# Third layer of a hybrid transformer on one core: attention heads issued in pairs, and negated scores in all layers

## What is computed

```python
def _masked_softmax(s, mask):
    s = jnp.where(mask, s.astype(jnp.float32), NEG_INF)
    m = jnp.max(s, axis=-1, keepdims=True)
    e = jnp.where(mask, jnp.exp(s - m), 0.0)
    return e / jnp.maximum(jnp.sum(e, axis=-1, keepdims=True), 1e-30)

def second_block(x, ...):
    ...
        h = _rms_norm(x, g_pre_mix[l]) * (1.0 + sc_m) + sh_m
        y = _hybrid_mixer(h, cos, sin, w_in[l], ...)
        x = x + ga_m * _rms_norm(y, g_post_mix[l])
        h = _rms_norm(x, g_pre_ffn[l]) * (1.0 + sc_f) + sh_f
        x = x + ga_f * _rms_norm(_swiglu(h, w_gate_up[l], w_down[l]), g_post_ffn[l])
```

## Time and profile before

| | us |
|---|---|
| median of 3 runs | 1135.73 |
| lowest, highest | 1133.7, 1137.04 |
| the profiled execution, its span | 1136.34, 1134.5 |

### The profile page before, as it was taken

The page is one execution under the profiler, slowest core; times in us unless marked ns, Lnnn a source line. Parts: engine busy times, 40 slices in busy tenths (PEclk is TensorE's granted clock), DMA queues, the critical chain, the costliest instruction groups (busy, mean ns, idle before and its releaser), DMA issues.

```text
span 1134.5 us, 16103 instructions
## 1 busy us (share of the span) xinstructions
PE 1039.9 (92%) x6560; PEld 926.6 (82%) x6560; DVE 684.4 (60%) x1268; ACT 446.4 (39%) x699; POOL 48.0 (4%) x70
## 2 busy tenths in 40 slices
PE   6999869999999899977999999889989859999997
PEld 5877659999988888756999988688766649999986
DVE  3656565777755755456777774756754555555543
ACT  4445323333333355423433333354444354333332
POOL 5100010000000200001000000100000000000000
PEclk9998998999999999898999999989987988999999
DMA  8733028998854553205999864454320025666551
GB/s 269 231 132 111 1 75 260 276 271 246 282 188 125 174 185 120 67 22 167 276 278 261 268 234 165 136 179 149 112 75 1 1 75 149 186 185 186 186 185 38
DMA packets 191706, 185.09 MB, mean 163 GB/s; under 512 B 7130, under 2 KB 161013, under 8 KB 191632
## 3 DMA queue, kind: packets, MB, share of 16 engines
q1 hardware_dynamic: 188576, 175.85, 50.4%
q0 software_dynamic: 2768, 7.87, 2.4%
q10 hardware_dynamic: 288, 0.33, 0.1%
HBM read 182.97 MB, written 1.06 MB: 162 GB/s over the span
## 4 chain that ended last, share of the span: by engine, by line
PE 79%; DVE 12%; ACT 5%; issue 2%; POOL 1%; DMA 1%; SPq 0%; DVEq 0%; POOLq 0%; ACTq 0%
PE ps L979 14%; PE ps L1020 11%; PE ps L1021 11%; PE ps L1022 11%; PE ps L1337 5%; PE ps L957 4%; PE ps L958 4%; PE ps L959 4%; PE ps L1064 3%; DVE wl L1694 3%; PE ps L1074 2%; ACT wh L1455 1%; DVE probs L1907 1%; DMA raw<-in_w_in 1%; ACT probs L1479 1%
## 5 line engine op out<-in xcount | busy, mean ns | idle before, releaser
L1694 DVE TENSOR_TENSOR wl<-raw,wh 128x2048 fp32r<-128x2048 f32 (+5 forms) x147 | 319.6, 2177 | 212.9 <-ACT wh L1455 212.7
L1455 ACT ACTIVATE wh<-raw 128x2048 fp32r<-128x2048 f32 (+5 forms) x147 | 268.1, 1824 | 438.1 <-PE ps L1022 247.6
L1020 PE MATMUL ps<-xh,wh 128*128 128x256 f32 x1056 | 303.1, 287 | 3.3 <-DVE xl L1712 2.0
L1021 PE MATMUL ps<-xl,wh 128*128 128x256 f32 x1056 | 302.0, 286 | 0.0
L1022 PE MATMUL ps<-xh,wl 128*128 128x256 f32 x1056 | 301.8, 286 | 0.0
L1020 PEld LDWEIGHTS ps<-xh,wh 128*128 128x128 f32 x1056 | 206.1, 195 | 4.4 <-issue 4.4
L1021 PEld LDWEIGHTS ps<-xl,wh 128*128 128x128 f32 x1056 | 206.1, 195 | 0.0
L1022 PEld LDWEIGHTS ps<-xh,wl 128*128 128x128 f32 x1056 | 206.0, 195 | 0.0
L957 PE MATMUL ps<-wh,xh 128*128 128x384 f32 (+5 forms) x284 | 106.2, 374 | 12.8 <-DVE wl L1694 7.1
L959 PE MATMUL ps<-wh,xl 128*128 128x384 f32 (+5 forms) x284 | 100.0, 352 | 0.0
L958 PE MATMUL ps<-wl,xh 128*128 128x384 f32 (+5 forms) x284 | 100.0, 352 | 0.0
(11 more groups left out here) (260 smaller groups left out, 1219.5 us busy)
## 6 DMA issues: line engine op xcount, KB each, us to landing
raw<-in_w_down SPq DMA_DIRECT2D x33, 1024.0 KB, 5.0
adaw<-in_w_ada SPq DMA_DIRECT2D x24, 1024.0 KB, 7.1
raw<-in_w_gate SPq DMA_DIRECT2D x44, 512.0 KB, 4.2
raw<-in_w_up SPq DMA_DIRECT2D x44, 512.0 KB, 5.5
raw<-in_w_gate_up SPq DMA_DIRECT2D x44, 512.0 KB, 5.1
raw<-in_w_in SPq DMA_DIRECT2D x12, 768.0 KB, 4.6
raw<-in_w_in SPq DMA_DIRECT2D x8, 1024.0 KB, 5.2
raw<-in_w_o SPq DMA_DIRECT2D x8, 1024.0 KB, 4.9
```

Source lines behind the costliest of these rows:

```text
L1020: mm(o, a[:, v, k, :], xh[:, k, :], start=k == 0, stop=False)
L1021: mm(o, a[:, v, k, :], xl[:, k, :], start=False, stop=False)
L1455: me.go(activation(wh[:, m % NW, 0:n], raw[:, ITEM[item] % NRAW, 0:n], ACT.Copy), wh_ready)
L1694: me.go(V.tensor_tensor(wl[:, m % NW, 0:n], raw[:, ITEM[item] % NRAW, 0:n], wh[:, m % NW, 0:n].bitcast(F32), ALU.subtract), wl_ready)
```

## The change

Third layer: jobs of the first two groups alternate between the two key heads (0, 4, 1, 5, 2, 6, 3, 7), so that two neighbouring jobs read partitions 0 to 63 and 64 to 127. A stage "S2" makes the scores of two jobs, the first row block of both and then the second of both, in banks 4 and 0. The transposes of odd jobs go to bank 2 (jobs below 8) or 1. `pair(p)` adds S2 of pair p, V of the two jobs of pair p-2, whatever stands between, and T of pair p-1. Block 5 is cut into 16 pieces "wq" of three products, spread among the first pairs. The latent group's results go to banks 6 and 7, the output product to banks 2, 3, 0, 1; the window result is now added last. The latent queries' turns go to banks 1 and 0. In all layers `masked` scales by the negative, takes the running minimum and does no negation; `exponents` uses a scale of -1.

```diff
-        for h in range(8):
+        for h in (0, 4, 1, 5, 2, 6, 3, 7):
...
-OBANK = {0: {0: 6, 1: 2, 2: 6}, 1: {0: 6, 1: 2, 2: 6}, 2: {0: 6, 1: 2, 2: 2, 3: 6}}
+OBANK = {0: {0: 6, 1: 2, 2: 6}, 1: {0: 6, 1: 2, 2: 6}, 2: {0: 6, 1: 2, 2: 6, 3: 6}}
...
-YBANK = {0: (0, 1, 2, 3), 1: (0, 1, 2, 3), 2: (0, 1, 6, 7)}
+YBANK = {0: (0, 1, 2, 3), 1: (0, 1, 2, 3), 2: (2, 3, 0, 1)}
...
-    def job(s, jobs=24):
-        add(*((n, k) for n, k in (("T", s - 2), ("V", s - 3), ("S", s)) if 0 <= k < jobs))
+    def fifth(a, b):
+        add(*(("wq", n // 8, n // 4 % 2, n % 4) for n in range(a, b)))
+
+    def pair(p, between=(), jobs=24):
+        if 2 * p < jobs:
+            add(("S2", 2 * p))
+        add(*(("V", k) for k in (2 * p - 4, 2 * p - 3) if k >= 0))
+        add(*between)
+        add(*(("T", k) for k in (2 * p - 2, 2 * p - 1) if 0 <= k < jobs))
...
+    fifth(0, 4)
     add(("wl", "win", 4, 1), ("nT", 0), ("nT", 1), ("top", 1))
...
+    fifth(4, 6)
+    pair(0)
+    fifth(6, 8)
+    add(("wh", "win", 5, 0), ("top", 2))
+    pair(1, [("wq", 1, 0, 0)])
+    fifth(9, 10)
     add(("wl", "win", 5, 0))
...
+    pair(2, [("wq", 1, 0, 2), ("wq", 1, 0, 3)])
+    add(("top", 3))
+    pair(3, [("wq", 1, 1, 0), ("wq", 1, 1, 1)])
+    add(("top", 4))
+    pair(4, [("wq", 1, 1, 2), ("wq", 1, 1, 3)])
+    add(("wh", "win", 5, 1), ("latent_query_rope",), ("cmpS",))
+    pair(5)
+    add(("cmpT",), ("wl", "win", 5, 1), ("out", 0, 0), ("out", 0, 1), ("top", 5))
+    pair(6, [("nT", 2), ("nT", 3)])
+    add(("top", 6), ("top", 7))
+    pair(7, [("cmpV",)])
+    add(("top", 8))
+    pair(8)
+    add(("out", 3, 0), ("out", 3, 1), ("out", 3, 2), ("out", 3, 3))
+    pair(9)
+    add(("out", 1, 0), ("out", 1, 1), ("out", 1, 2), ("out", 1, 3))
+    pair(10)
+    pair(11, [("ht", 0, 0), ("ht", 0, 1)])
+    pair(12, [("wo", 0, 0), ("wo", 1, 0)])
+    pair(13, [("wo", 2, 0), ("wo", 3, 0)])
...
-                put(("nT", a[0]), a[0] - 2, "act")
+                put(("nT", a[0]), 3 - a[0], "act")
...
+            elif stage == "S2":
+                put(("s", L, a[0]), 4, "dve")
+                put(("s", L, a[0] + 1), 0, "dve")
...
-                put(("pt", L, a[0]), 5, turns(L, a[0]))
+                other = L == 2 and a[0] % 2
+                put(("pt", L, a[0]), (2 if a[0] < 8 else 1) if other else 5, turns(L, a[0]))
...
+            def two_scores(k):
+
+                j = JOBS[2][k]
...
+                banks = [claim(("s", 2, k)), claim(("s", 2, k + 1))]
+                for t in range(TT):
+                    for n in range(2):
+                        ins = score(JOBS[2][k + n], banks[n], t)
+                        if t:
+                            fill(ins, ("s", 2, k + n))
...
-                wide = P if not j.last and (j.col + 2) * HD <= 512 else HD
+                wide = P if (j.col + 2) * HD <= 512 and not j.last and (j.kind not in ("slc", "win") or j.col != 3) else HD
...
-                    ins = activation(probs[:, k % 4, a:e], probs[:, k % 4, a:e], ACT.Exp, bias=nmx[:, k % 4, t:t + 1],
+                    ins = activation(probs[:, k % 4, a:e], probs[:, k % 4, a:e], ACT.Exp, bias=mn[:, k % 4, t:t + 1], scale=-1.0,
...
-                    me.go(V.tensor_tensor_reduce(out=probs[:, k % 4, a:e], in0=ps[:, U.bank[key], a:e], in1=mask_of(j, t), scale=j.scale,
-                                                 scalar=-3.4e38, op0=ALU.add, op1=ALU.max, accum_out=mx[:, k % 4, t:t + 1]))
-                me.settle()
-                me.empty(V.tensor_scalar(nmx[:, k % 4, :], mx[:, k % 4, :], -1.0, None, ALU.mult), key)
+                    ins = V.tensor_tensor_reduce(out=probs[:, k % 4, a:e], in0=ps[:, U.bank[key], a:e], in1=mask_of(j, t), scale=-j.scale,
+                                                       scalar=3.4e38, op0=ALU.add, op1=ALU.min, accum_out=mn[:, k % 4, t:t + 1])
+                    if t:
+                        me.empty(ins, key)
+                    else:
+                        me.go(ins)
```

More of the change, by code:

```diff
@@ L941, in first_part, with fifth_part @@
                     mm(o, xh[:, k, 0:P], b[:, k, :], start=False, stop=False)
+            def fifth_part(h, t, k):
+                n = win_width(2, 5)
+                a, b = (w[:, 0:4 * n].rearrange("p (k n) -> p k n", k=4) for w in parts(("win", 2, 5, h)))
+                if h == k == 0:
+                    claim(("win", 2, 5, t))
+                o = ps[:, U.bank["win", 2, 5, t], 0:n]
+                xs = slice(t * P, (t + 1) * P)
+                mm(o, xh[:, 4 * h + k, xs], a[:, k, :], start=h == k == 0, stop=False)
+                mm(o, xh[:, 4 * h + k, xs], b[:, k, :], start=False, stop=False)
+                ins = mm(o, xl[:, 4 * h + k, xs], a[:, k, :], start=False, stop=h == 1 and k == 3)
+                if k == 3:
+                    if h == 1:
+                        fill(ins, ("win", 2, 5, t))
+                    elif t == 1:
+                        leave(ins, ("win", 2, 5, h))
             def win_part(L, i, h, t):
@@ L1046, in scores @@
                 b = claim(("s", L, k))
-                if L == 2 and j.col == 0:
-                    for key in {"slc": (("nT", 0), ("nT", 1), ("nT", 4)), "win": (), "dsa": (("nT", 2), ("nT", 3), ("nT", 7), ("nT", 8))}[j.kind]:
-                        wait_done(pe, key)
-                if k == 0 and L < 2:
+                if k == 0:
                     wait_done(pe, ("ab", L, 0))
@@ L1545, in mixer @@
                 for stage, *a in ORDER[L]:
-                    if stage == "win" and a[1:] == [1, 0]:
+                    if stage == "wq" and a == [1, 0, 3]:
+                        key = ("win", 2, 5, 0)
+                        copy(*win_views(2, 5, 0, win_width(2, 5), U.bank[key]), key)
+                    elif stage == "S2":
+                        exponents(L, a[0])
+                        exponents(L, a[0] + 1)
+                    elif stage == "win" and a[1:] == [1, 0]:
                         key = ("win", L, a[0], 0)
@@ L2178, in mixer @@
                 for stage, *a in ORDER[L]:
-                    if stage == "win" and a[1:] == [1, 1]:
+                    if stage == "wq" and a == [1, 1, 3]:
+                        key = ("win", 2, 5, 1)
+                        copy(*win_views(2, 5, 1, win_width(2, 5), U.bank[key]), key)
+                    elif stage == "S2":
+                        masked(L, a[0])
+                        masked(L, a[0] + 1)
+                    elif stage == "win" and a[1:] == [1, 1]:
                         key = ("win", L, a[0], 1)
```

67 lines of the change are left out of this document (19 added, 48 removed).

## The result

| | before | after |
|---|---|---|
| median of 4 runs, us | 1135.26 | 1108.43 |
| lowest, highest | 1133.7, 1137.04 | 1107.61, 1112.77 |
| the profiled execution, its span | 1136.34, 1134.5 | 1109.17, 1107.4 |
| mean granted clock of TensorE | 0.963 | 0.971 |

The ratio is 0.976, with an interval of 0.974 to 0.978.

A forecast was written before the change was run, and what follows sets the result against it. TensorE was taken as the bound (79% of the chain), losing time to waits and low clock in the third layer. 21.8 (work and waits at full clock) - 6 (clock) + 2 (first layers) = 17.8 us: 1118 us, range 1109 to 1129.

The forecast's parts named there:

- work of TensorE less: Third layer: a pair of heads costs 2.95 us against 4.02 for two single heads; twelve pairs save 12.8 us.
- change of waits: Third layer's new stretch: TensorE waits 13.2 us in place of 12.1.
- loss to the clock, from 10.1: Third layer: some 14 us at half clock, costing 6 us after one hidden; bounds nothing and the 10 us of before.
- layers one and two: Dropping the negation shortens six waits per layer by 0.2 us each: 2 us taken; bounds nothing and 8 us.
- the first rival: The clock stays full in the third layer's stretch: gain 21.8 + 2, 1112 us; chance 0.18.
- place 4: Latent queries' second turn waits 2.4 us for bank 0 until head 13 is masked; scores 14 then wait 1.25 us.
- All five places: Third layer's late spots: first values, scores 10, compressed transposes, latent turn with scores 14, last third; together 13.2 us.
- the walk: Stepping the third layer's new order once through three engines with assumed durations; no waits in steady state, 13.2 us in all.
- The two forms without a row: Running minimum in the mask and scale of -1 in the exponent: no difference taken; 0.05 us a head would be 3 us.
- the second rival: Third layer's paired scores don't overlap when interleaved: 0.85 us more a pair, 7 us after waits hide a third; 1125 us; chance 0.12.
- VectorE and ScalarE did not become the bound: Rival that they would, in the third layer: 10 us of waiting on top, 1128 us; chance 0.12.
- the low clock did not hold on: Rival that it would: 1.2 GHz for all of the third layer's stretch, 17.6 us longer, 1152 us; chance 0.04.

The follow-up runs named there:

- four late masks: The kernel after with one unneeded VectorE product (about 1.2 us) ahead of each mask of jobs 16, 18, 20 and 22; 1112.06 us.
- doubled compressed scores: The kernel after with the compressed score products made twice (16 more products of 32 columns, same result); 1109.25 us.
- both heads in the same rows: The kernel after with jobs of the selected and window groups in order 0 to 7, so paired heads have keys in the same partitions; 1115.45 us.
- the late masks: The kernel after with unneeded VectorE products: 2.4 us ahead of job 12's mask (1113.45 us), or 1.2 us ahead of four later masks (1112.06 us).

## Why the prediction was right or wrong

The gain in the profiled executions is 27.1 us (1134.5 to 1107.4). Block 5's first product starts at 810.99 before and 808.08 after, so 2.9 us come from ahead of block 5, and 24.2 from the third layer's stage; after the second turn of heads nothing more is won or lost (907.78 to 880.71, and the end likewise). Against the steps (work, waits and clock by windows with other rounding, 0.1 us less in sum):

| step | forecast, us | measured, us |
|---|---|---|
| work of TensorE less | 12.8 | 10.2 |
| change of waits | 1.1 more | 3.8 less |
| loss to the clock, from 10.1 | 6 left | 0 left |
| layers one and two | 2 | 2.9 |
| gain | 17.8 | 27.0 |

*The clock was the step that failed.* "I expect a low stretch after them and another in the last third" did not come: the row of the whole stretch reads 1.00. That was the first rival, at 0.18. It was worth 6 us of the 9.3 missed. The reason given, that waits in lumps lower the clock, is partly right: one wait made longer by 2.5 us, or block 5 taken from between the heads, brought low stretches right behind the idle time in the profiled executions. What failed is the size: the lumps were smaller than walked (1.9 and 0.8 us at place 4, not 2.4 and 1.25), and 2.3 idle us in 6.8 did not lower the clock here, while with four late masks 2.4 in 6.8 did and 2.6 did not. Busy time doesn't protect either, as the doubled compressed scores show. The rule that low rows follow idle rows was taken from two rows of one execution, and it was too thin to place a stretch by. Why the clock stayed full through the whole stage is not shown.

*The waits were over-counted.* All five places exist, in the order walked. Measured and forecast: first values 1.20 and 1.8; scores 10 for bank 4 0.66 and 0.9; compressed transposes 0.95 and 1.3; latent turn 1.87 and 2.4; what follows it 0.77 and 1.25 (it fell on the transposes of the next pair, behind the copy of the same turn, and not on scores 14); the last third 3.15 and 5.5. Together 8.6 and 13.2: each is 0.6 to 0.8 of the walk. Which duration or hand-over of the walk was too long was not tried. The waits of before were also not all of single heads, as the prediction reads the earlier trace rows: 2.0 us are for VectorE's pass over a group's outputs (L1851) and 2.0 for the copy of the compressed attention's turned probabilities (`bias`), so 8.1 of 12.1 are. Two of the waits, in the timeline:
```profile
820.83 0.46 PE L1127 MATMUL ps<-proj,pT 128*128 128x128 f32 x2 [1.20 <-ACT pT L1481]
...
844.83 0.63 PE L1236 MATMUL ps<-cst,proj 128*128 128x128 f32 x4 [1.87 <-DVE mn L1948]
```
Taken with the clock, these two steps are 10.9 us of the miss.

*The work was over-counted, by 2.6 us.* A pair costs 3.05 us and not 2.95, which is 1.2 us over twelve pairs. The scores' overlap was right to the digit (0.93 us). The measured 10.2 us are 78.6 less 10.1 of clock less 59.7 in the two windows, 8.8, and 1.4 from the part between block 5's first product and the first scores (6.4 to 5.0 us), whose six products now stand between heads. The other 1.4 us of the miss I can't place by line.

*Negated scores.* The forecast of 2 us for the first two layers stands against 2.9 in the trace, which is less than two executions of one kernel can differ by there. Over the table, block 5 begins at 809.6 us in the mean of the three kernels with the negation and at 807.0 in that of the eleven without, some 2.6 us. Layer one's waits fell from 3.5 to 2.6 us, not to 2.3. In runs, negation undone costs 3.8 us, 7.4 at full clock, over all three layers; the waits show half of the latter. Where the other half sits stays open. The two forms without a row cost nothing, as taken.

*Block 5 in pieces* had no price in the prediction. It hides no waits in sum; the 2 to 4 us that it seems to be worth come by the clock. *The loads and splits of the output weights* moved without being late: the second turn of heads is 27.1 us earlier, like the end.

*The other rivals.* Pairs overlap (0.93 us), interleaved or not, so the second rival fell. Taken away in eight of twelve pairs, the overlap costs 7 us in the median, the figure that the rival had for twelve, but by luck: 4.4 of the 5.1 us go into waits, the clock makes up the rest, and part of that clock is ahead of the stage. VectorE and ScalarE did not become the bound, and the low clock did not hold on.

*What the prediction did not see* is how much hangs on the second transpose bank. It was counted within the walk and not by itself. The walk held that in the steady state nothing waits; with one bank twelve transposes wait 14.4 us. Without it 15.5 us of the 27 are lost, 6.8 us at full clock and the rest by the clock. With single heads the one bank cost only 5.1 us of waits for copies of heads, so most of this wait is made by the pairs and then taken away by the bank. The costs of the parts taken away one by one need not add up to 27.

*What stays open:* what makes the clock fall where TensorE is busy for nine tenths of the window before. It differs between executions of one kernel: 58 or 80 us of low-clock time with both heads in the same rows, 1107.6 or 1112.8 us for the kernel after. That the third layer's stage has no low stretch in the profiled execution of after is seen; that it never has one is not.

## What to carry to other kernels

Before placing a low-clock stretch in a forecast, read the granted clock of several windows with like idle shares: if some fell and some did not, as here (2.3 us idle of 6.8 without, 2.4 with), give the clock term its full bounds, here 0 to 10 us, and hold the range open to "none". Price each bank or buffer of a loop by itself, as what waits if it alone were taken away: here leaving out the second transpose bank costs 15.5 us of the 27, and leaving out the halves of the array, the more striking part, 1 us at full clock. Before giving a difference of a few us to a change, compare the stage itself in the profiles and the stages that were not changed: here the latter moved by up to 6 us. Waits walked came out too long here (the measured ones were 0.6 to 0.8 of the walk), so keep the lower end of the range open to less.

## What the runs showed of the hardware

- Score products in rows 0 to 63 and 64 to 127 overlap just as well when four of one kind stand before four of the other: 0.93 us for eight either way, 1.57 us in the same rows.
- With work that fills idle time the low stretch of 13.6 us behind it was gone in the profiled execution, and one of 17.1 us came later, where no filler was.
- A window of code that is the same in both kernels, with the same idle time, ran at 1.00 in one execution and at 0.83 in another (layer two, 455 to 475 us, 18.41 us busy of 20 in both).
- The low clock (0.50, that is 1.2 GHz) came after windows with TensorE busy for 0.90 of the time (both heads in the same rows, compressed scores twice), and did not come after one busy for 0.66 (the kernel after, from 837.5), nor after one busy for 0.61 (four late masks, from 837.5). The Trainium skill, TensorE: Matmul & The Clock Gate, section A second HAM failure mode: psum-queue depth-cycling, puts one such swing down to small pauses between groups of products; the late masks agree with it (idle 3.0 of 6.9 us, then 10.2 us low), the compressed scores don't bear it out as the only cause.
